# A two-block network on one core: the last pair of feed-forward chunks written out, its gated rows turned in the middle of a down projection

## What is computed

```
def swiglu(h, w1, w3, w2):
    return (jax.nn.silu(h @ w1) * (h @ w3)) @ w2

x = x + mod_l[5] * swiglu(modulate(rmsnorm(x, ffn_norm_g[i]), mod_l[3], mod_l[4]),
                          ffn_w1[i], ffn_w3[i], ffn_w2[i])
```

## Time and profile before

| | us |
|---|---|
| median of 3 runs | 1022.97 |
| lowest, highest | 1019.21, 1023.39 |
| the profiled execution | 1023.64 |
| its span, first to last instruction | 1022.0 |
| PE busy in the span | 924.2 (90%) |
| DVE busy | 738.4 (72%) |
| ACT busy | 471.2 (46%) |
| POOL busy | 137.3 (13%) |
| mean granted clock of PE, share of full speed | 0.963 |

### The profile page before, as it was taken

The page is one execution under the profiler, slowest core; times in us unless marked ns, Lnnn a source line. Parts: engine busy times, 40 slices in busy tenths (PEclk is TensorE's granted clock), DMA queues, the critical chain, the costliest instruction groups (busy, mean ns, idle before and its releaser), DMA issues.

```text
span 1022.0 us, 12453 instructions
## 1 busy us (share of the span) xinstructions
PE 924.2 (90%) x4323; PEld 725.5 (71%) x4323; DVE 738.4 (72%) x1065; ACT 471.2 (46%) x774; POOL 137.3 (13%) x203
## 2 busy tenths in 40 slices
PE   3799987779999999899988999999978998999986
PEld 0588754666888888677566788888856876777764
DVE  0696488688787768579668787768687888885455
ACT  1542256435344343462175444343445775455451
POOL 0000002134110131030102310111001200101000
PEclk9899999889999999999979999999979999999998
DMA  9978155367999898637615698898836444965001
GB/s 354 376 283 279 51 182 174 106 234 228 387 312 316 285 332 281 217 129 247 205 64 191 228 345 309 288 311 293 311 124 223 148 169 162 348 228 186 1 21 41
DMA packets 119046, 229.09 MB, mean 224 GB/s; under 512 B 8650, under 2 KB 64684, under 8 KB 119002
## 3 DMA queue, kind: packets, MB, share of 16 engines
q1 hardware_dynamic: 92608, 141.57, 40.1%
q0 software_dynamic: 24224, 86.32, 24.4%
q10 hardware_dynamic: 2170, 0.64, 0.3%
HBM read 227.43 MB, written 1.08 MB: 224 GB/s over the span
## 4 chain that ended last, share of the span: by engine, by line
PE 68%; DVE 16%; ACT 6%; issue 5%; DMA 2%; POOL 1%; ACTq 0%; POOLq 0%; SPq 0%; DVEq 0%
PE bank L1850 20%; PE bank L1852 19%; PE bank L1851 19%; DVE w_lo L1148 4%; DVE job_sum L1165 2%; ACT w_hi L656 2%; DMA w_land<-ev_w_in_dram 2%; PE bank L2368 1%; DVE x L1230 1%; DVE tmp L1229 1%; DVE mx L1366 1%; PE bank L2209 1%; PE bank L1928 1%; DMA ident<-k_ident_dram 1%; ACT xfull L965 1%
## 5 line engine op out<-in xcount | busy, mean ns | idle before, releaser
L1850 PE MATMUL bank<-w_hi,xT_hi 128*128 128x512 f32 x816 | 332.8, 408 | 21.1 <-DVE xT_lo L1274 9.5
L1148 DVE TENSOR_TENSOR w_lo<-w_land,w_hi 128x2048 fp32r<-128x2048 f32 x114 | 260.9, 2294 | 98.2 <-ACT w_hi L656 98.1
L1851 PE MATMUL bank<-w_lo,xT_hi 128*128 128x512 f32 x816 | 323.4, 396 | 0.0
L1852 PE MATMUL bank<-w_hi,xT_lo 128*128 128x512 f32 x816 | 323.0, 396 | 0.0
L656 ACT ACTIVATE w_hi<-w_land 128x2048 fp32r<-128x2048 f32 x116 | 221.7, 1914 | 117.6 <-PE bank L1852 115.0
L1850 PEld LDWEIGHTS bank<-w_hi,xT_hi 128*128 128x128 f32 x816 | 156.8, 192 | 62.7 <-issue 22.1
L1852 PEld LDWEIGHTS bank<-w_hi,xT_lo 128*128 128x128 f32 x816 | 156.4, 192 | 34.4
L1851 PEld LDWEIGHTS bank<-w_lo,xT_hi 128*128 128x128 f32 x816 | 156.7, 192 | 30.2
L1165 DVE SCALAR_TENSOR_TENSOR job_sum<-a_land,silu_c,job_sum 128x1024 f32<-128x1024 f32 x126 | 163.3, 1296 | 6.1 <-DMA a_land<-mod_w_dram 3.1
L1850 PE MATMUL bank<-w_hi,hT_hi 128*128 128x512 f32 x176 | 70.6, 401 | 3.3 <-DVE hT_lo L1508 3.3
L1851 PE MATMUL bank<-w_lo,hT_hi 128*128 128x512 f32 x176 | 69.2, 393 | 0.0
(11 more groups left out here) (315 smaller groups left out, 1096.3 us busy)
## 6 DMA issues: line engine op xcount, KB each, us to landing
w_land<-ffn_w_dram SPq DMA_DIRECT2D x132, 512.0 KB, 5.8
a_land<-ada_w_dram POOLq DMA_DIRECT2D x40, 1024.0 KB, 5.9
a_land<-mod_w_dram POOLq DMA_DIRECT2D x24, 1024.0 KB, 5.7
w_land<-od_pw_w_dram SPq DMA_DIRECT2D x24, 512.0 KB, 5.0
w_land<-ev_w_in_dram SPq DMA_DIRECT2D x20, 512.0 KB, 12.9
w_land<-ada_w_dram SPq DMA_DIRECT2D x16, 512.0 KB, 10.9
a_land<-kv_mod_w_dram POOLq DMA_DIRECT2D x8, 1024.0 KB, 6.7
w_land<-rg_w_in_dram SPq DMA_DIRECT2D x16, 512.0 KB, 5.9
```

The costliest lines, as they stand in the source:

```text
L1148: dve.tensor_tensor(w_lo[u % N_SPLIT][:, :], w_land[n % N_LAND][:, :], w_hi[u % N_SPLIT][:, :].bitcast(F32), ALU.subtract).then_inc(s_lo, 1)
L1850: pe.matmul(dst, hi, whi, start=start, stop=False)
L1851: pe.matmul(dst, hi, wlo, start=False, stop=False)
L1852: return pe.matmul(dst, lo, whi, start=False, stop=stop)
```

## The change

The last pair of chunks (c = 9 and 10) is written out behind a loop of four rounds, on PE and ACT in both layers and on DVE in layer 1 (in layer 0 it was already). In the written-out pair, down(9) takes the turn of chunk 10 after four of its eight groups of three matmuls. Since down(9) still reads `hT_hi` and `hT_lo` then, the turned rows of chunk 10 go to a second place, `last_hi` and `last_lo` (2 KB per partition each), which down(10) reads. On DVE `hidden_lo` of chunk 10 moves ahead of `split_lo`, and in layer 1 the two halves of job unit 3 stand together behind it. SP and POOL are as before.

```
+        last_hi = place("last_hi", [P, 2, S], BIG + 40 * KB, R32)
+        last_lo = place("last_lo", [P, 2, S], BIG + 42 * KB, R32)
...
 ACT
-                for q, n in loops:
-                    with act.Fori(0, n) as i:
-                        for b in range(2):
...
+                def pair(done, q, i, dst=hT_hi):
+                    for b in range(2):
...
+                        split_hi(u + 4, i)
+                        hidden_hi(c, i, dst if b == 1 else hT_hi)
+
+                with act.Fori(0, loops - 1) as i:
+                    pair(0, first_job, i)
+                pair(loops - 1, first_job + loops - 1, None, last_hi)
...
 DVE
                         if b == 1 - layer:
+                            if b == 1 and i is None:
+                                hidden_lo(c, i, last_hi, last_lo)
+                                split_lo(u + 4, i)
+                                job_cols(q, i)
+                                continue
...
                         else:
                             job_units(q + layer, (2,), i)
+                            if b == 1 and i is None:
+                                hidden_lo(c, i, last_hi, last_lo)
+                                split_lo(u + 4, i)
+                                job_units(q + layer, (3,), i)
+                                continue
                             split_lo(u + 4, i)
                             if layer == 1:
                                 job_units(q + 1, (3,), i, (0,))
                             hidden_lo(c, i)
                             job_units(q + layer, (3,), i, range(layer, 2))
...
+                with dve.Fori(0, loops - 1) as i:
+                    pair(0, first_job, i)
+                pair(loops - 1, first_job + loops - 1, None)
...
 PE
-                def down(c, u, i=None, last=False):
+                def down(c, u, i=None, last=False, between=None):
                     unit_wait(u, i)
+                    hi, lo = (last_hi, last_lo) if last else (hT_hi, hT_lo)
...
                     for n, (k, h, t) in enumerate(order):
+                        if n == 4 and between is not None:
+                            between()
...
+                        if b == 1 and i is None:
+                            down(c - 1, u + 2, i, between=lambda: turn_hidden(c, i))
+                        else:
                             down(c - 1, u + 2, i)
                             turn_hidden(c, i)
+                        if b == 1 - layer:
+                            job_turn(q, i)
+
+                with pe.Fori(0, loops - 1) as i:
+                    pair(0, first_job, i)
+                pair(loops - 1, first_job + loops - 1, None)
```

More of the change, by code:

```diff
@@ L914, in ffn @@
                 hidden_hi(0)
-                done = 0
-                for q, n in loops:
-                    with act.Fori(0, n) as i:
-                        for b in range(2):
[L919 to L928, removed]
+                def pair(done, q, i, dst=hT_hi):
+                    for b in range(2):
+                        u = base + 2 + 6 * done + 3 * b
+                        c = 1 + 2 * done + b
+                        split_hi(u + 2, i)
+                        split_hi(u + 3, i)
+                        silu(c, u, i)
+                        if b == 1 - layer:
+                            job_copy(q, i)
+                        split_hi(u + 4, i)
[3 more added lines that the diff above has]
+                pair(loops - 1, first_job + loops - 1, None, last_hi)
                 split_hi(base + 3 * FCH + 1)
                 half_squares(("n_pw1", "n_rg")[layer], 4 + 8 * layer, (0, 1, 2), tiles_first=True)
-            ffn(0, [(4, 5)], 4)
+            ffn(0, 5, 4)
             def spectrum_out(c):
@@ L1517, in ffn, with pair @@
                 job_units(first_job, range(2) if layer == 0 else range(2, 4))
-                def pair(done, q, i, following=True):
+                def pair(done, q, i):
                     for b in range(2):
@@ L2195, in down @@
                     for n, (k, h, t) in enumerate(order):
-                        ins = three(bank[2 + 2 * h + t][:, :], hT_hi[:, k, t * P:t * P + P],
-                                    hT_lo[:, k, t * P:t * P + P], wh[:, k, 512 * h:512 * h + 512],
+                        if n == 4 and between is not None:
+                            between()
+                        ins = three(bank[2 + 2 * h + t][:, :], hi[:, k, t * P:t * P + P],
+                                    lo[:, k, t * P:t * P + P], wh[:, k, 512 * h:512 * h + 512],
                                     wl[:, k, 512 * h:512 * h + 512], False, last and k == 1)
@@ L2220, in ffn, with pair @@
                     pe.matmul(bank[2 + n][:, :], zeros[0:1, 0:P], zeros[0:1, :], start=True, stop=False)
[L2221 to L2229, removed]
+                def pair(done, q, i):
+                    for b in range(2):
+                        u = base + 2 + 6 * done + 3 * b
+                        c = 1 + 2 * done + b
+                        up(c, u, i)
+                        if b == 1 - layer:
+                            job_sums(q, i)
+                        if b == 1 and i is None:
+                            down(c - 1, u + 2, i, between=lambda: turn_hidden(c, i))
+                        else:
                             down(c - 1, u + 2, i)
                             turn_hidden(c, i)
-                            if b == 1 - layer:
-                                job_turn(q, i)
-                    done += n
+                        if b == 1 - layer:
+                            job_turn(q, i)
+                with pe.Fori(0, loops - 1) as i:
+                    pair(0, first_job, i)
+                pair(loops - 1, first_job + loops - 1, None)
                 pe.wait_ge(sem("hid"), 2 * (off + FCH))
                 down(FCH - 1, base + 3 * FCH - 1, None, True)
-            ffn(0, [(4, 5)], 4)
+            ffn(0, 5, 4)
             def turn_pair(stage, src, free):
@@ L2354, in _ @@
             dense("pw2", 2, "ln", mid=gate_mid("pw2"), norm_after="n_ffn1")
-            ffn(1, [(10, 5)], 10)
+            ffn(1, 5, 10)
             def rg_gate_mm(g):
```

25 lines of the change are left out of this document (8 added, 17 removed).

## The result

The changed kernel took 1028.53 us (median of 7 runs, six of them between 1026.84 and 1028.94) beside 1022.97 us (7 runs, 1019.21 to 1025.6) of the kernel before. The ratio is 1.0051 with a 95% interval of 1.0035 to 1.0067. It is slower by some 5 us; 1022.3 had been predicted, with a range up to 1024.9. One of its runs took 5142.57 us; it and two like it further on (1560.33 us of the kernel before, 4186.1 us of e8) stand in no ratio. The profiled execution took 1028.94 us, with a span of 1027.3 us.

A forecast was written before the change was run, and what follows sets the result against it. The prediction saw PE as 68% of the chain, but DVE's and ACT's order ahead of the residuals as limiting the gain; 0.4 + 0.2 = 0.6 us off 1022.97 gave 1022.3 us, range 1018.4 to 1024.9.

The forecast's parts named there:

- the pair that follows is the same work in straight code: Leaving the loops one round early on PE, ACT and DVE changes no work; counted as nothing.
- POOL is not touched: In layer 1, POOL's next load that waits for job sums has others to wait for in the stage behind.
- The turn on PE: Chunk 10's transposes (0.44 us) go inside down(9), first matmul behind them 0.08 us longer; PE then waits for nothing before down(10).
- Layer 0: 0.4 us predicted: ACT's w_hi copy starts at about 421.12 instead of 421.53; half split and residuals move 0.4 us earlier.
- as costed: Layer 0's full weight split on DVE runs 1.9 us later, delaying SP's load; both costed at nothing.
- Layer 1: 0.2 us predicted: DVE stands 0.19 us for hT_hi; the second residual no longer waits 0.35 us for PE; 0.2 us gained.
- The clock: Layer 1's down(10) runs at full speed, about 1.7 us gained, and ends some 3.5 us earlier on PE.
- The scatter: PE's slow stretches behind the two norms, 1.5 to 2.5 us each, shift the time up to 1 us either way.
- PE's gain passing through whole: Rival: PE's gain in both layers, together 4.8 us, reaches the total, giving 1018.2 us; chance 0.07.
- Instruction fetch: Rival: PE's loop exits cost 3.3 us for fetching the straight pair, giving 1025.6 us; chance 0.08.
- DVE held at hT_lo: Rival: a late turn or ACT delays DVE's queue in layer 1; 2 us of delay gives 1023.7; chance 0.06.
- The turn not starting in the middle: Rival: the rows to be turned are late and PE's gap stays, giving 1023.0 us; chance 0.03.

The follow-up runs named there:

- e8: The changed kernel, count 8, with ACT again copying and counting job 8's rows in layer 0's written-out pair; 1020.71 us, ratio 0.9965.
- e4: e1 with the last two job sums of layer 1 moved on DVE into the next stage; 1021.22 us, ratio 0.9976.
- e6: e4 with the half weight split moved behind the second residual on DVE in both layers; 1020.55 us, ratio 0.9975.
- e1: The changed kernel with POOL waiting for seven kept rows instead of eight before job 12's gate row; 1021.83 us, ratio 0.9990.
- e2: The kernel before with POOL waiting for nine kept rows instead of eight, nothing else changed; 1031.09 us, ratio 1.0072.
- e3: The changed kernel with count 7, but the turn behind down(9) and DVE's order as before; 1023.75 us, ratio 1.0001.
- e7: e6 with the turn behind down(9) and DVE's order as in e3; 1020.57 us, ratio 0.9962.

## Why the prediction was wrong, point by point

**The step that failed** is "the pair that follows is the same work in straight code", and with it "POOL is not touched". It isn't the same work: i = None is also the switch by which `job_copy` leaves out a copy and a count. I took the written-out pair for a matter of loop exits and ranged it at nothing to 2.0 us per exit on PE, an engine that had nothing to do with it, and took nothing. The price was about 7.2 us ("layer 1" of after against e8, which differ by that copy alone), three engines away: ACT's count, POOL's wait of 24.18 us, the weight loads queued behind it, DVE's 9.12 us, PE's 4.57 us and 2.4 us at half clock. None of the rivals contained it.

**The turn on PE was right.** After shows it at 419.07, behind the twelfth matmul of down(9), which began at 416.21:

```profile
419.07 0.60 PE L2221 MATMUL bank<-ident,hid 128*128 128x128 f32 x4
419.43 0.47 PE L1859 MATMUL bank<-w_hi,hT_hi 128*128 128x512 f32 x1
419.74 0.39 PE L1860 MATMUL bank<-w_lo,hT_hi 128*128 128x512 f32 x1
...
422.39 0.48 PE L1859 MATMUL bank<-w_hi,last_hi 128*128 128x512 f32 x1
```

It takes 0.36 us (0.44 reckoned) and the first matmul behind it 0.08 more, as estimated. Down(10) starts without idle. The wait on hT_lo is gone in both layers.

**Layer 0: 0.4 us predicted, 0.39 measured** (15.72 to 15.33). ACT's copies and DVE's half split behind them, which answer to the earlier trace rows:

```profile
419.70 0.60 ACT L910 ACTIVATE last_hi<-bank 128x512 fp32r<-128x512 f32 x1 [1.17 <-PE bank L2221]
422.51 1.92 ACT L658 ACTIVATE w_hi<-w_land 128x2048 fp32r<-128x2048 f32 x1 [2.21 <-PE bank L1861]
```

```profile
424.46 1.23 DVE L1266 TENSOR_TENSOR w_lo<-w_land,w_hi 128x1024 fp32r<-128x1024 f32 x1 [1.16 <-ACT w_hi L658]
425.61 0.68 DVE L1234 TENSOR_TENSOR tmp<-bank,gate 128x512 f32<-128x512 f32 x1
```

The copy starts 6.76 us behind the last silu, before 7.17, and waits for PE's last use of the buffer, not for hT_hi. The full split stands 1.87 us later on DVE (5.19 against 3.32 us behind the silu). Only SP waits longer for such splits (15.6 us between 410 and 440 us, before 8.6), and up to 470 us no engine waits for a weight load, as costed.

**Layer 1: 0.2 us predicted, 0.11 measured** (17.78 to 17.67). DVE stood 0.11 us ahead of last_lo (0.19 reckoned), and has no other pause up to the first residual. That one starts 10.65 us behind the last silu, 0.33 later than before (0.19 forecast), and the second 11.99 us behind it, 0.09 earlier (0.16 forecast):

```profile
745.40 2.60 DVE L1170 SCALAR_TENSOR_TENSOR job_sum<-a_land,silu_c,job_sum 128x1024 f32<-128x1024 f32 x2
748.11 0.69 DVE L1513 TENSOR_TENSOR last_lo<-bank,last_hi 128x512 fp32r<-128x512 f32 x1
748.71 2.28 DVE L1153 TENSOR_TENSOR w_lo<-w_land,w_hi 128x2048 fp32r<-128x2048 f32 x1
750.91 2.60 DVE L1170 SCALAR_TENSOR_TENSOR job_sum<-a_land,silu_c,job_sum 128x1024 f32<-128x1024 f32 x2
753.43 1.22 DVE L1266 TENSOR_TENSOR w_lo<-w_land,w_hi 128x1024 fp32r<-128x1024 f32 x1
```

The reading that the queue, not PE, sets this place was confirmed by taking work off it: e4 gained 1.17 us and e6 another 1.82.

**The clock.** Down(10) of layer 1 ran at full clock, where the earlier trace rows had 0.58 and 0.56. Its last matmul starts 3.8 us earlier against the last silu (10.95 instead of 14.79 us), where the prediction had 3.5:

```profile
748.00:750.00 2.00, 2.00 (x10) 1.66 (x9) 1.90 (x2) 0.07 (x1) 0.00 (x0) 1.00 0.42 157
750.00:752.00 2.00, 2.00 (x10) 1.65 (x10) 2.00 (x2) 1.69 (x1) 0.00 (x0) 1.00 0.00 0
```

PE then idles 7.14 us, and the transposes come out at half clock, as said. From e1:

```profile
761.29 1.97 PE L1898 MATMUL bank<-ident,xn 128*128 128x128 f32 x8 [7.14 <-DVE xn L1259]
```

1.97 us instead of 1.12, and hidden: the rest of the kernel took 265.0 us against 265.2. This is what the advice against long gaps between bursts of matmuls is about (the Trainium skill, "TensorE: Matmul & The Clock Gate", section "Why this matters for your kernels"). The trace agrees on the drop; it cost nothing at this place.

**The scatter** is what I mis-sized. I took the slow stretches, in which PE is at half clock, for noise of up to 1 us either way. In the table they come in steps that mostly belong to the kernel: the kernels with the old end of layer 0 (before, e2, e3) have a convolution stage of 118.7 us each time and, where no stall comes in, 190.2 us in layer 1; six of the other ten profiled executions have 117.4 to 117.6 us, and the five of these without a stall have 188.6. Together that is 2.8 us, more than the 0.5 us that the turn moves at its two places, and it fits the medians: e1 is 1.9 us under e3, e8 3.3 us under before.

In layer 1 the step is the clock's. Windows of PE near the start of that stretch, of before and then of e8 at the same place (its stretch starts 1.46 us earlier):

```profile
570.00:575.00 5.00, 5.00 (x16) 0.66 0.29 73
```

```profile
568.00:573.00 5.00, 5.00 (x23) 1.00 0.24 77
```

Before is at half clock for 5 x 0.34 x 2 = 3.4 us there, which is worth 1.7 us of work, and the stretch is 1.59 us longer. In the convolution stage the granted clock, summed over windows of 2 us, gives 17.1 us at half clock in before and 10.2 in e8. Half of that difference is 3.5 us, but the stage is only 1.1 us shorter: PE idles 11.4 us of it in e8 and 9.4 in before, so the clock explains this step only in part. For e1's two executions it is 23.9 and 10.2 us, half of the difference 6.9 us, of the 7.2 us in length.

The steps are not fixed to a kernel. Each run has a mean granted clock. Of the 43 runs of before beside e1 and e8, five had 0.966 or more, and these took 1020.40 to 1021.02 us; the other 38 took 1021.82 us and more. The five runs of e8 all had 0.968 and took 1019.72 to 1021.13 us, while e1 had 0.966 or more in five of 12. So the kernel before can have the short pattern too and then takes as long as e8, but it seldom has it. Why 0.4 us less at the end of layer 0 makes another pattern more frequent is not settled by these runs.

**The rivals.** PE's gain passing through whole (1018.2) fell in this kernel. Once DVE was out of the way (e6 against e7) the turn gave 3.2 of these 4.8 us at its two places, and no gain in the total. Instruction fetch (1025.6) had the right sign by accident, and e3 refutes it. DVE held at hT_lo: 0.11 us, nothing. (Its price was added up wrongly too: a delay of 2 us on a forecast of 1022.3 gives 1024.3, not 1023.7.) The turn not starting in the middle: refuted by the rows.

**A faster version.** e6, e7 and e8 are at 1020.6, 1020.6 and 1020.7 us, each faster than the kernel before, by 3.3 to 3.5 us of the medians taken beside it; after was 5.6 us above before. These three cannot be ranked by their medians.

## What to carry to other kernels

When the last round of a loop is written out, compare the work of the straight copy with a round of the loop instruction by instruction: each condition on the loop register is a possible change, and each semaphore that it counts has waits elsewhere, against absolute numbers, perhaps on an engine and in a stage that the diff doesn't show. Comparing the instruction counts by engine (774 to 772) finds such a thing at once. A wait that becomes one count too strict costs only time as long as the count is still reached, and here the eighth of eight copies reached it. It shows first where the queue behind it runs dry. And before a PE gap is closed, ask which queue starts the next step: here 3.3 us of idle were worth 0.5 us, since DVE's order held the residuals, and in layer 0 ACT's weight copy behind down(9) did.

## What the runs showed of the hardware

PE's clock went to half in a stretch in which PE had been busy without a pause for some 9 us, the last 3.3 us of them with matmuls on 31 of the 128 rows or of 8 columns. It did so at the same place in three of three executions of one kernel and in none of two of its neighbour, which has the same small matmuls. The same kernel, e1, had 124.64 us in one execution and 117.46 in another for the same stage, with 23.9 and 10.2 us at half clock. So a difference of 7 us between two profiles of one kernel can come from this: read the granted clock of the stages before you compare two single profiles of this kernel.
